# Rounding streamed weights four chunks ahead of TensorE on ScalarE, while VectorE makes their lower parts three chunks ahead

## The reference, cut to what matters

```
mod = silu(c) @ w_ada + b_ada ; shift, scale, gate = split(mod)
z = (rms_norm(x) * (1 + scale) + shift) @ w_in          # 1024 x 2976
...                                                     # attentions
x = x + gate * (y @ w_out)
...
h = h + 0.5 * rmsnorm(swiglu(rmsnorm(h), w_gu, w_down)) # 1024 x 5632, 2816 x 1024
h = h + rmsnorm(mixer(rmsnorm(h)))                      # w_in_2 1024 x 6912, w_branch, w_out_2
```

## Time and profile before

| what | value |
|---|---|
| median of 3 runs | 1725.86 us (1724.89 to 1728.15) |
| the profiled execution's own time | 1725.93 us |
| its span, first to last instruction | 1724.1 us |
| mean granted TensorE clock | 0.981 |
| busy in the span | PE 94%, DVE 62%, ACT 49%, POOL 7% |
| DMA | 293 MB, mean 170 GB/s |

### The profile page before, as it was taken

The page is one execution under the profiler, slowest core; times in us unless marked ns, Lnnn a source line. Parts: engine busy times, 40 slices in busy tenths (PEclk is TensorE's granted clock), DMA queues, the critical chain, the costliest instruction groups (busy, mean ns, idle before and its releaser), DMA issues.

```text
span 1724.1 us, 21793 instructions
## 1 busy us (share of the span) xinstructions
PE 1616.7 (94%) x7796; PEld 1328.2 (77%) x7796; DVE 1069.9 (62%) x1792; ACT 845.4 (49%) x1487; POOL 119.9 (7%) x157
## 2 busy tenths in 40 slices
PE   1789989899999999999999999999999999999998
PEld 1667777777888787877778887888778787778886
DVE  5787677666565646567675656565555556766653
ACT  0355645645444565555464445444455655464442
POOL 3011001100000300001100000000020000200000
PEclk9987989999999999999999999999999999999999
DMA  9584256335555553444656555555583353655552
GB/s 280 199 282 140 84 184 218 110 123 178 188 186 194 152 177 117 134 135 146 203 173 193 181 196 182 186 177 195 154 229 93 113 171 104 200 190 188 176 195 78
DMA packets 155336, 293.27 MB, mean 170 GB/s; under 512 B 10214, under 2 KB 23316, under 8 KB 155228
## 3 DMA queue, kind: packets, MB, share of 16 engines
q1 hardware_dynamic: 149312, 276.60, 50.0%
q0 software_dynamic: 4800, 12.29, 3.0%
q10 hardware_dynamic: 1116, 2.99, 0.5%
HBM read 290.77 MB, written 1.06 MB: 169 GB/s over the span
## 4 chain that ended last, share of the span: by engine, by line
PE 77%; DVE 10%; ACT 5%; issue 4%; DMA 2%; POOL 1%; SPq 0%; DVEq 0%; POOLq 0%; ACTq 0%
PE pb L433 72%; PE pb L437 4%; ACT wh L803 2%; DVE wl L1290 2%; DMA raw<-in_w_ada 2%; DVE acc L1287 1%; POOL st L2041 1%; ACT p L803 1%; ACT pb L803 1%; DVE xt_l L1287 1%; DVE ti L1287 1%; ACT xt_h L803 1%; ACT ti L803 1%; DVE dg L1284 0%; DMA raw<-in_w_in 0%
## 5 line engine op out<-in xcount | busy, mean ns | idle before, releaser
L1290 DVE TENSOR_TENSOR wl<-raw,wh 128x1024 fp32r<-128x1024 f32 (+1 forms) x484 | 576.3, 1219 | 337.2 <-ACT wh L803 333.3
L803 ACT ACTIVATE wh<-raw 128x1024 fp32r<-128x1024 f32 (+1 forms) x484 | 496.0, 1051 | 264.7 <-PE pb L433 222.6
L433 PE MATMUL pb<-wh,xt_h 128*128 128x512 f32 (+2 forms) x1536 | 597.2, 389 | 13.0 <-ACT wh L803 11.0
L433 PE MATMUL pb<-wl,xt_h 128*128 128x512 f32 (+2 forms) x1536 | 588.7, 383 | 15.2 <-DVE wl L1290 15.1
L433 PE MATMUL pb<-wh,xt_l 128*128 128x512 f32 (+2 forms) x1536 | 588.9, 383 | 0.7 <-DVE xt_l L1287 0.4
L433 PEld LDWEIGHTS pb<-wh,xt_h 128*128 128x128 f32 x1536 | 294.2, 192 | 69.9 <-ACT xt_h L803 11.7
L433 PEld LDWEIGHTS pb<-wl,xt_h 128*128 128x128 f32 x1536 | 294.3, 192 | 69.4 <-DVE wl L1290 18.9
L433 PEld LDWEIGHTS pb<-wh,xt_l 128*128 128x128 f32 x1536 | 293.8, 191 | 59.9 <-DVE xt_l L1287 5.7
L433 PE MATMUL pb<-wh,big_h 128*128 128x512 f32 x352 | 138.7, 394 | 0.0
L433 PE MATMUL pb<-wl,big_h 128*128 128x512 f32 x352 | 138.6, 394 | 0.0
L433 PE MATMUL pb<-wh,big_l 128*128 128x512 f32 x352 | 136.7, 388 | 0.0
(11 more groups left out here) (205 smaller groups left out, 1492.9 us busy)
## 6 DMA issues: line engine op xcount, KB each, us to landing
raw<-in_ffn_w_gu SPq DMA_DIRECT2D x176, 512.0 KB, 4.6
raw<-in_w_in SPq DMA_DIRECT2D x148, 512.0 KB, 4.3
raw<-in_ffn_w_down SPq DMA_DIRECT2D x88, 512.0 KB, 4.4
raw<-in_w_ada SPq DMA_DIRECT2D x48, 512.0 KB, 5.4
raw<-in_w_out SPq DMA_DIRECT2D x32, 512.0 KB, 4.0
raw<-in_w_branch SPq DMA_DIRECT2D x24, 512.0 KB, 3.7
raw<-in_w_in SPq DMA_DIRECT2D x8, 416.0 KB, 4.2
G<-in_na_rpb POOLq DMA_DIRECT2D x32, 96.0 KB, 8.6
```

The lines of the kernel that those rows point to most:

```text
L433: return e.matmul(o, a, b, start=start, stop=stop)
L803: return e.activation(o, a, func, **kw)
L1290: return e.tensor_tensor(o, a, b, op)
```

## The change

`Stream` gets its distance as an argument. ACT's stream uses AHEAD + 1 = 4, DVE's keeps AHEAD = 3. No buffer, no transfer and no arithmetic changes, and neither ring changes its size.

```diff
@@ class Stream
-    def __init__(self, plan):
-        self.plan, self.taken, self.next, self.freed = plan, 0, 0, 0
+    def __init__(self, plan, ahead):
+        self.plan, self.ahead, self.taken, self.next, self.freed = plan, ahead, 0, 0, 0
@@ Stream.take
-            if split is not None and not (split <= c + AHEAD and split - NW < self.freed):
+            if split is not None and not (split <= c + self.ahead and split - NW < self.freed):
@@ act
-        stream = Stream(plan)
+        stream = Stream(plan, AHEAD + 1)
@@ dve
-        stream = Stream(plan)
+        stream = Stream(plan, AHEAD)
```

## The result

| | before | after |
|---|---|---|
| median | 1725.86 us (1724.38 to 1728.15, 6 runs) | 1707.52 us (1704.92 to 1712.27, 6 runs) |
| ratio, 95% interval | | 0.9896 [0.988, 0.9913] |
| span of the profiled execution | 1724.1 us | 1708.4 us |
| mean granted clock in it | 0.981 | 0.989 |

The change makes the kernel 18 us faster. The prediction said 1719.4 us, in a range of 1708 to 1733: the sign was right, the size too small by 12 us, and the result lies just outside the range.

The account below looks back on a forecast made before the run. PE, busy 94% of the span, was taken as the bound. Gains of 12.0 us and losses of 4.6 + 2.9 + 1.9 + 2.6 gave 0.0 idle time; clock -6.5 made 1725.93 into 1719.4 us, range 1708 to 1733.

Parts of the forecast that it names:

- Gain 1: `diff` attention: the rounding leaves the ring of ACT and DVE, PE's waits for `p` shrink; 5.8 us of idle time.
- Gain 2: Attention in block 1: PE's waits shrink by 3.7 us, those for ACT's copies by 1.5; rotary stretches in mixers give 1.
- the clock in block 1: Low stretches: at 305 half of 3.4 us returns, at 134 a quarter of 6.9; at 97 nothing changes.
- The clock term: Whole kernel: low-clock stretches partly go, new ones cost 2 us; net -6.5 us, between -15 and +10.
- Loss 1: Layer 0, qb to kb: a late load ahead of the evacuation lengthens PE's wait from 6.9 to 11.5 us; 4.6 us.
- Loss 2: Layer 0, end of vb: rounding chunk 19 ahead of the evacuation delays the first `qt` copy; 2.9 us.
- Loss 3: Layer 1, qb to kb: a chunk landing near 265.3 delays DVE's subtraction past PE's need; 1.9 us.
- Loss 4: Mixers, end of va: one more chunk ahead of the evacuation delays head copies; 1.0 us in the first, 1.6 in the second.
- What should have shown it: Signs: DVE's `wh` wait below 120 us, `p` wait below 1, 94 us wait 11.5, new waits near 125 and 275.
- B (nothing moves): Whole kernel: DVE's waiting is hidden, gains and losses cancel and the clock stays; 1726 us, chance 0.20.
- A (late transfers win): ACT's list in block 1: the copy for c+4 stands for its load ahead of evacuations; slower, 1732 us, chance 0.22.
- C (the clock returns in full, losses 2 and 3 hidden): All low stretches but the first disappear, -15 instead of -6.5 us, and two losses are hidden; 1706 us, chance 0.08.

Follow-up runs that it names:

- experiment 3: The changed kernel with ACT back to three chunks ahead from z to vb in block 1 and from qa to va in the mixers; 1697.19 us.
- experiments 7 and 8: First: the changed kernel with DVE four chunks ahead too, 1731.8 us. Second: the kernel before with DVE two ahead, ACT still three, 1707.42 us.
- experiment 6: The kernel before with one blank line more, run for a second profile; 1724.21 us.
- block 2 alone: The kernel before with ACT four chunks ahead in block 2 only, three in block 1; 1713.19 us.
- experiment 14: The changed kernel with sixteen DVE copies of 128x512 into an unused tile ahead of one combination in the first `diff` attention; 1714.2 us.
- experiments 4 and 12: First: the kernel before, ACT four ahead only in z to vb, qa to va; 1737.38 us. Second: the change, rounding behind evacuations and copies there; 1698.13 us.
- experiment 2: The kernel before with ACT four chunks ahead in block 1 only, three in block 2; 1720.75 us.
- Experiment 10: The changed kernel with ACT evacuating before it rounds in every slot with a product's last chunk; 1750.01 us.

## Why the prediction was right in sign and wrong in size

The sum on record was: gains 12.0 us of idle time and 8.5 of clock, losses 12.0 of idle time and 2 of clock, net 0.0 of idle time and -6.5 of clock. Measured on PE, the first pair of profiles has -1.2 us of idle time and -15.6 of clock (with PE busy), the second -6.3 and -9.8, in the mean -3.7 and -12.7. So the term that failed is first the clock, taken at half its size, and second the idle time, where the gains outweighed the losses.

Cut by place instead of by kind, experiment 3 measures the gains without the losses: 27.8 instead of 20.5 us. Its difference to the change measures the losses: 10.3 instead of 14.0 us. The two errors, 7.3 and 3.7 us, point the same way and make the 11 to 12 us. One loss did not come.

**Gain 1, `diff`: right.** I took 5.8 us of idle time plus 5.1 of clock, 10.9. The steps in the change are 5.5 (775 to 805) and 6.4 (1350 to 1475), 11.9 in all. The reason, a ring through ACT's exponentials, rounding, DVE's subtraction and combination, is shown by experiments 7 and 8. The wait of DVE in the earlier trace rows is gone: DVE's timeline has `762.20 1.22 DVE L1290` without a bracket.

**Gain 2 and the clock in block 1: too small.** I took 3.7 + 1.5 us of idle time and, of the clock, half of the stretch at 305 and a quarter of that at 134, 8.6 us together. Experiment 3 is 13.8 us ahead at the end of block 1. The step that failed is the one where I let the stretch at 97 last "as long past the restart as now" and let go only a quarter of that at 134, "since work there is thin in any case". Past the restart the first lasted 9.3 us in the kernel before (5.8 in its second profile) and 3.0 in the kernel after (3.8). DVE's wait for `wh` between 130 and 180 us was 13.1 us in the trace of before and has no line in that of after: that part of layer 0 was in the same ring as `diff`. That the clock came back because of it is not shown: experiment 6 shows 3.4 us less lost at 134 for the unchanged kernel, and the trace with block 2 alone has no low stretch there, though its block 1 is that of before. Nor are all of the 13.8 us an effect of the change, since the second trace of before is itself 3.4 us ahead of the first at that place.

**The clock term as a whole: mis-sized.** Stretch by stretch, with PE busy, in the two pairs of profiles: at 97 forecast nothing, given back 3.1 and 1.0 us; at 134 forecast 1.7, given back 5.1 and 3.3; at 305 forecast 1.7, given back 3.4 and 3.4; behind the `diff` waits forecast 5.1, given back 5.1 and 5.1. Against these stand new stretches, forecast 2, measured 1.7 us (at 329) in the first pair and 5.4 (at 53, 84 and 327) in the second. What the second pair has beyond these is mostly the stretch at 1345 of the kernel before, 3.4 us, which neither profile of after has. The price that I used, the length of a stretch times one minus its clock, holds where PE is busy: experiment 14 lost 1.65 us where that product is 4 x 0.43 = 1.7. Where PE waits through part of the stretch it is too high: at 97 it gives 6.9 us and PE's busy time 4.6. What was wrong is how many I let go.

**Loss 1, qb to kb: right in kind, 3.3 instead of 4.6 us.** The chain came as set down, 1.1 to 1.3 us earlier at each link: the chunk ahead of the evacuation was rounded from 93.12, not from 94.2, and the subtraction ended PE's wait at 104.92 instead of 101.64. PE's wait was 9.1, forecast 11.5. And it cost almost nothing further on: at 111 us the change is only 0.3 us behind, since the clock, low until 111 in the kernel before, was full from 108.

**Loss 2, end of vb: right, and short.** 3.54 us for `qt`, forecast 2.9. I missed the 1.19 us at 119.57, a subtraction that comes late because ACT had stood 10.00 us for a load until 110.86, ahead of the squares and the rotary factors.

**Loss 3, layer 1: did not come.** ACT's timeline of the kernel after:

```profile
263.41 1.06 ACT L803 ACTIVATE wh<-raw 128x1024 fp32r<-128x1024 f32 x1 [3.29 <-DMA raw<-in_w_in]
264.38 1.06 ACT L803 ACTIVATE qkv<-pb 128x512 f32<-128x512 f32 x2
266.40 1.17 ACT L803 ACTIVATE th<-qkv 128x512 f32<-128x512 f32 x2
```

The load was issued at 259.79 and landed within 3.6 us; I had taken 5.0 and a later issue, for 265.3. The evacuation was 1.2 us late and the squares, at 266.40 against 266.10, only 0.3. The one number for loads was the error: I should have taken the row's low end where few transfers are under way. Over the busy stretch of layer 0 (59 to 125 us) the median from issue to landing was again 5.7 us.

The Trainium skill, DMA: Bandwidth & Descriptors, section "Anatomy of one DMA", has a fit for descriptors made by software, from which the prediction's estimates of 3.2 us for such a load and 0.2 us for this loss come. The measured 3.6 us and the absent wait are nearer to these than to my 5.0 and 1.9; the 5.7 us of layer 0 are not. The page of the profile lists these loads as hardware_dynamic, a path that this fit is not made for.

**Loss 4, mixers: right for the first, half for the second.** 1.22 and 0.84 us, forecast 1.0 and 1.6.

**What should have shown it.** The waits for `p`, the stretches at 779 and 1442 and the unchanged feed-forward parts came as said (0.04 us between 400 and 600). The wait near 94 us grew and the one near 125 us appeared, the first to 9.1 us and not to 11.5; the one near 275 us did not come. DVE's wait for `wh` fell to 204 us and not below 120. Between 368 and 600 us it is 39.0 us before and 41.3 after: there DVE has nothing else to do and arrives early at any distance. That wait was never a measure of the ring, and I should have asked for it in the attention stretches alone.

**The rivals.** B (nothing moves) is refuted by the result. A (late transfers win) has its mechanism, a rounding for c+4 that stands for its load ahead of evacuations and copies: experiments 4 and 12 show it as 11.8 and 9.4 us. It did not decide, because the gains were 28 us and not the 6 to 10 that A gave them. C (the clock returns in full, losses 2 and 3 hidden) at 1706 us was nearest to the time, in part by luck; of its reasons the clock came for the greater part (12.7 us in the mean, of its 15) and loss 3 was hidden, loss 2 was not.

## What to carry to other kernels

When two engines split one piece of work in the same slot (here: ACT rounds, DVE subtracts), put one slot between them: what then leaves the loop is the wait of the second engine, and it doesn't matter which of the two is moved (1707.5 and 1707.4 us), while moving both alike gains nothing (1731.8 us). In a list that is worked through strictly in order, look at what a prefetch stands ahead of: the same early rounding cost some 10 us where its load came late and an evacuation and a copy stood behind it, and nothing once it stood behind them. Choose the distance by stretch. And when you count what a wait of TensorE costs, remember that low clock may stand behind it, and count that only where TensorE is busy.

## What the runs showed of the hardware that was not expected

A single wait of PE of 3.48 us, put into a stretch at full clock, was followed by 4 us at clock 0.57 in the mean, near the lower of the two levels (1.2 and 2.4 GHz), though PE was busy throughout (experiment 14). The 2.07 us wait of the earlier trace rows had the same behind it, but that is not a rule without exception. Five traces have a wait of about 2 us there; in four a low stretch followed (1.7 us lost in two, 3.4 in two), and in that of experiment 7 none, though the wait was 2.08 us. In the second mixer the same five have waits of 2.05 to 2.09 us, again four with a low stretch; there the exception is experiment 2. Experiment 10 has the same at other places: none of the waits of 1.5 us at the ends of parts had a low stretch in any trace, each of its five of 5.8 us had one. This row of experiment 7 begins at the end of its wait:

```profile
779.00:787.00 8.00, 7.63 (x37) 5.80 (x38) 4.40 (x14) 4.61 (x12) 0.43 (x1) 1.00 0.32 100
```

The low stretches are not a fixed property of a kernel. Two profiles of the kernel before lost 29.7 and 25.9 us to them with PE busy (33.5 and 30.8 by length), two of the kernel after 14.1 and 16.1 (18.6 and 23.9), with medians of the time within 1.7 us for each pair. The Trainium skill, TensorE: Matmul & The Clock Gate, Part 1, says of the slow matmuls at a kernel's start that their number is "run-variable"; these traces show that low stretches in the middle of a kernel vary too. So the clock term of one profile is uncertain by 2 to 4 us, up to a fifth of this change's effect, and what of it belongs to which edit stays open for block 1.
